# Four overflow blocks of an expert loop, moved from its end to places between its groups

## The reference, cut to what matters

```
def hier_moe(h, w_rg, b_rg, w_re, b_re, w_gate, w_up, w_down):
    ...                                  # choose 1 of 4 groups, then 2 of its 8 experts per token
    comb = jnp.einsum('tk,tke->te', gate, jax.nn.one_hot(eidx, N_EXPERTS, dtype=jnp.float32))
    a = jnp.einsum('td,edf->tef', t, w_gate)
    b = jnp.einsum('td,edf->tef', t, w_up)
    act = jax.nn.silu(a) * b * comb[:, :, None].astype(t.dtype)
    y = jnp.einsum('tef,efd->td', act, w_down)
```

## Time and profile before

| | |
|---|---|
| median of 3 runs | 1477.09 us (1475.53 to 1477.17) |
| the profiled execution's own time | 1473.9 us |
| its span in the trace | 1472.1 us |
| PE busy | 1273.6 us (87%) |
| DVE busy | 775.6 us (53%) |
| ACT, POOL busy | 283.2 us (19%), 150.3 us (10%) |
| DMA moved | 238.27 MB, mean 162 GB/s |
| expert loads (gate, up, down) | 36 of each, 1024 KB each |
| the loop, first gate-up product to the end of the last down product | 1061.19 to 1429.1 us |

### The profile page before, as it was taken

The page is one execution under the profiler, slowest core; times in us unless marked ns, Lnnn a source line. Parts: engine busy times, 40 slices in busy tenths (PEclk is TensorE's granted clock), DMA queues, the critical chain, the costliest instruction groups (busy, mean ns, idle before and its releaser), DMA issues.

```text
span 1472.1 us, 17784 instructions
## 1 busy us (share of the span) xinstructions
PE 1273.6 (87%) x6455; PEld 651.0 (44%) x6455; DVE 775.6 (53%) x2215; ACT 283.2 (19%) x812; POOL 150.3 (10%) x205
## 2 busy tenths in 40 slices
PE   7979699999999947787999999998599998899970
PEld 3435445554554433353555565655333433333430
DVE  1116789999898994231344445544435224434416
ACT  1123224433433341030111111111001110110100
POOL 0000001001100000100000000000100022132104
PEclk9998799999999968798999999998599999999995
DMA  8695000300000030372115110002379999999916
GB/s 329 245 351 181 1 22 1 143 30 16 14 29 15 1 141 29 128 264 115 29 43 215 43 43 15 1 15 100 127 297 384 356 407 418 417 416 416 389 67 222
DMA packets 68320, 238.27 MB, mean 162 GB/s; under 512 B 14112, under 2 KB 28358, under 8 KB 54387
## 3 DMA queue, kind: packets, MB, share of 16 engines
q1 hardware_dynamic: 56235, 217.20, 38.5%
q0 software_dynamic: 11424, 17.85, 3.5%
q10 hardware_dynamic: 576, 2.10, 0.4%
HBM read 216.27 MB, written 45.77 MB: 178 GB/s over the span
## 4 chain that ended last, share of the span: by engine, by line
PE 71%; DVE 13%; DMA 6%; issue 5%; ACT 2%; POOL 1%; SPq 1%; DVEq 0%; ACTq 0%; POOLq 0%
PE bank L777 24%; PE bank L1194 11%; PE bank L1147 9%; PE bank L1201 7%; DVE W L1605 6%; PE bank L976 3%; DMA W<-in_w_exp_down 3%; PE bank L1125 2%; PE bank L1085 2%; PE bank L820 2%; PE bank L1181 2%; DVE G L1550 1%; PE bank L889 1%; PE bank L1161 1%; DMA W<-in_cache_mem_k 1%
## 5 line engine op out<-in xcount | busy, mean ns | idle before, releaser
L777 PE MATMUL bank<-W,G 128*128 128x512 f32 (+3 forms) x864 | 354.0, 566 | 4.2 <-DVE G L1550 3.4
L1605 DVE SCALAR_TENSOR_TENSOR W<-W,dwT 128x128 f32<-128x128 f32 (+1 forms) x1080 | 280.3, 337 | 0.0
L777 PEld LDWEIGHTS bank<-W,G 128*128 128x128 f32 (+1 forms) x864 | 158.6, 187 | 176.2 <-issue 170.0
L1194 PE MATMUL bank<-W 128*32 128x512 f32 (+1 forms) x1600 | 204.9, 612 | 15.9 <-issue 14.2
L976 PE MATMUL bank<-W 128*128 128x512 f32 (+1 forms) x288 | 129.9, 610 | 11.7 <-DVE W L1711 7.8
L1194 PEld LDWEIGHTS bank<-W 128*32 128x32 f32 (+1 forms) x1600 | 65.4, 116 | 150.8 <-issue 148.4
L1147 PE MATMUL bank<-W 128*128 128x512 f32 (+1 forms) x288 | 128.2, 599 | 0.8 <-DVE W L1875 0.6
L659 POOL TENSOR_SCALAR st<-st 128x1 f32<-128x1 f32 (+5 forms) x58 | 13.2, 228 | 948.9 <-DVE st L1681 276.4
L1201 PE MATMUL bank<-W 128*32 128x512 f32 (+1 forms) x800 | 105.9, 610 | 4.1 <-DMA W<-in_w_exp_down 3.0
L2046 DVE TENSOR_TENSOR W<-bank,cvec 128x512 f32<-128x512 f32 x56 | 36.3, 687 | 131.3 <-PE bank L1181 131.2
L976 PEld LDWEIGHTS bank<-W 128*128 128x128 f32 (+1 forms) x288 | 54.0, 190 | 81.8 <-issue 81.6
(11 more groups left out here) (287 smaller groups left out, 1350.6 us busy)
## 6 DMA issues: line engine op xcount, KB each, us to landing
W<-in_w_exp_gate SPq DMA_DIRECT2D x36, 1024.0 KB, 11.5
W<-in_w_exp_up SPq DMA_DIRECT2D x36, 1024.0 KB, 15.6
W<-in_w_exp_down SPq DMA_DIRECT2D x36, 1024.0 KB, 15.5
y_scratch<-W SPq DMA_DIRECT2D x28, 512.0 KB, 12.7
y_scratch<-LG SPq DMA_DIRECT2D x1, 11264.0 KB
W<-in_cache_mem_k SPq DMA_DIRECT2D x8, 1024.0 KB, 5.3
W<-in_cache_mem_v SPq DMA_DIRECT2D x8, 1024.0 KB, 7.8
W<-in_w_in SPq DMA_DIRECT2D x4, 1792.0 KB, 25.1
```

The costliest lines, as they stand in the source:

```text
L777: mm = pe.matmul(bank[0:rows, at:at + hi - lo], HT[:, c, 0:rows], w[:, c, lo:hi], start=(c == 0), stop=(c == DC - 1))
L1194: mm = pe.matmul(B[2 + par][lo:hi, :], HG[par][:, c, lo:hi], WGU[u][:, :, c, :], start=(c == 0), stop=(c == DC - 1), skip_group_check=True)
L1605: dve.scalar_tensor_tensor(y, src, w, y, ALU.mult, ALU.add).then_inc(M["conv_tap"], 1)
```

## The change

The function `block_order` builds a list `BLOCKS`. It holds three expert blocks of each group, and behind the fourth, fifth, sixth and seventh group one overflow block. So the overflow blocks have the numbers 12, 16, 20 and 24 in the loop, and the last group's expert blocks are 25, 26 and 27. `block_column` gives the column of a block's rows in the index table, which keeps its old layout, and with it the place of its results in `y_d`. `weight_plan` walks the new order. The passes end with blocks 7 and 17 (7 and 15 before), and their combines go with blocks 10 to 15 and 20 to 25 (10 to 15 and 18 to 23 before). Two waits for the overflow table are added, on SP ahead of the read of an overflow block's expert number, and on GpSimd ahead of the first overflow block's row gather.

```
+def block_order():
+    order = []
+    for q in range(NE // 4):
+        order += [("e", 3 * q + r) for r in range(3)]
+        if 3 <= q < 3 + STATIC_OVER:
+            order.append(("o", q - 3))
+    return order
+
+
+BLOCKS = block_order()
+
+
+def block_column(n):
+    kind, k = BLOCKS[n]
+    return k if kind == "e" else NR + k
+
+
 def weight_plan():
-    need = []
-    for q in range(NE // 4):
-        need += [("e", 4 * q + 3)] + [("e", 4 * q + r) for r in range(3)]
-    need += [("o", k) for k in range(STATIC_OVER)]
-    uses = {}
-    for n in range(NR):
-        uses[n] = [("e", 4 * (n // 3) + n % 3), ("e", 4 * (n // 3) + 3)]
-    for k in range(STATIC_OVER):
-        uses[NR + k] = [("o", k)]
+    need, uses = [], {}
+    for n, (kind, k) in enumerate(BLOCKS):
+        if kind == "o":
+            uses[n] = [("o", k)]
+        else:
+            uses[n] = [("e", 4 * (k // 3) + k % 3), ("e", 4 * (k // 3) + 3)]
+        need += [w for w in reversed(uses[n]) if w not in need]
...
+        def pass_end(g):
+
+            return BLOCKS.index(("e", PER_PASS * (g + 1) - 1))
+
+        def stores_before(n, p):
+
+            return (n + 1 - p) // 2
+
         def comb_at(n):
 
-            g, j = n // PER_PASS - 1, 3 * (n % PER_PASS - 2)
-            return [] if g < 0 or g >= PASSES - 1 or j < 0 else [2 * NT * g + j + c for c in range(3)]
+            for g in range(PASSES - 1):
+                j = 3 * (n - pass_end(g) - 3)
+                if 0 <= j < 2 * NT:
+                    return [2 * NT * g + j + c for c in range(3)]
+            return []
...
                 if k not in over_e:
+                    sp.wait_ge(M["over_ready"], 1)
                     over_e[k] = sp.value_load(eid_i[0:1, k:k + 1], min_val=0, max_val=NE - 1)
...
-                gather(idx_i[:, n + 2:n + 3], zg_in[n % 2], ZG[n % 2])
+                if BLOCKS[n + 2] == ("o", 0):
+                    pool.wait_ge(M["over_ready"], 1)
+                at = block_column(n + 2)
+                gather(idx_i[:, at:at + 1], zg_in[n % 2], ZG[n % 2])
...
-                            pool.wait_ge(y_out[p], 16 * (PER_PASS // 2) * (g + 1))
+                            pool.wait_ge(y_out[p], 16 * stores_before(pass_end(g) + 1, p))
```

More of the change, by code:

```diff
@@ L597, in store_y @@
                 sp.wait_ge(M["yb_readyD"], n + 1)
-                g = min(n // PER_PASS, PASSES - 1)
-                sp.dma_start(y_d[g][(n - PER_PASS * g) * 128:(n - PER_PASS * g + 1) * 128, :], YB[n % 2]).then_inc(y_out[n % 2], 16)
+                at = block_column(n)
+                g = min(at // PER_PASS, PASSES - 1)
+                sp.dma_start(y_d[g][(at - PER_PASS * g) * 128:(at - PER_PASS * g + 1) * 128, :], YB[n % 2]).then_inc(y_out[n % 2], 16)
             over_e = {}
@@ L1184, in tiles_of @@
             def tiles_of(n):
-                if n >= NR:
+                if len(USES[n]) == 1:
                     return [(0, 128, WSLOT[USES[n][0]])]
```

## The result

| | before | after |
|---|---|---|
| median | 1477.59 us (7 runs, 1475.53 to 1481.47) | 1470.79 us (7 runs, 1467.23 to 1473.65) |
| profiled execution, its span | 1473.9, 1472.1 us | 1472.01, 1470.0 us |
| the loop, first gate-up to the end of the last down product | 1061.19 to 1429.14: 367.95 us | 1065.40 to 1425.89: 360.49 us |

The ratio of the changed kernel to the one before is 0.9949, with a 95% interval of 0.9933 to 0.9964: 6.8 us less. Two more comparisons of the same kernel gave 0.9935 (0.9908 to 0.9961) and 0.9954 (0.9937 to 0.9972). The forecast was 1469.6 us.

The account below looks back on a forecast made before the run. The full DMA stream was taken to bound the loop from 1178 us. Gain 9.7 - 1.7 - 0.5 = 7.5 us from the 1477.1 us median gave 1469.6 us, own range 1466 to 1473, wider range 1462.5 to 1475.5.

Parts of the forecast that it names:

- What bounds: Expert loop from 1178 us: the DMA byte stream, not TensorE, sets the pace; waits and slow products cost 22.3 us.
- check by bytes: Blocks 9 to 21 take 161.9 us, 140.2 without waits; their 66.62 MB need 160.5 us at 415 GB/s.
- The sum: Up to expert 28's weights: 48.6 us less TensorE work behind, 38.9 us more stream ahead; after small terms 7.5 us gained.
- main term of 9.7 us: Loop's end comes earlier by 48.6 us of TensorE work minus 38.9 us of added stream, before two small terms.
- The slow product at 25: Block 25's gate-up takes 8.77 instead of 7.05 us if TensorE waits over 3 us there: +1.7 us.
- The shape of the last blocks: Last three blocks become expert blocks of 32-column products, period 11.68 against 11.50 and 11.39 us: together +0.5 us.
- The small edits: SP's four expert-number reads (0.39 us each before), added overflow-table waits and moved combine gathers were costed at nothing.
- The signs: Right if DMA stays full until about 1380 us and waits sum to 12; wrong if loop's end moves under 4 us.
- an earlier issue doesn't make a full stream faster: For experts 17, 21 and 25, whose slots are freed three blocks ahead instead of two, no gain was counted.
- All waits go: Rival for TensorE's loop waits: longer issue distances clear them, gain up to 22.3 us, 1454.8 us; chance 0.10.
- The stream slows with the overflow loads in it: Rival for the loop's DMA: register-addressed loads run at 347 GB/s, no gain, 1477 us; chance 0.12 including moved waits.
- Late combine gathers: Rival for the second combine group: gathers landing after 20.7 us delay six steps by 2.0 us each, 1481.6 us; chance 0.06.

Follow-up runs that it names:

- the old order with the small loads: Kernel before, with the four overflow experts' loads cut to 64 columns of one chunk and no expert-number reads; ratio to before 0.9998, loop 368.85 us.
- the new one with them: Changed kernel, with the four overflow experts' loads cut to 64 columns of one chunk and no expert-number reads; ratio to before 0.9849, loop 347.34 us.
- the version with the pair behind the seventh group: Changed kernel with one overflow block moved from behind the sixth to behind the seventh group; ratio to before 0.9896, again 0.9919.

## Why the prediction was right

*What bounds.* Right: the stream sets the pace from 1178 us on. Without the overflow loads in it the waits went from 11.4 to 2.0 us. My "check by bytes" was none: 66.62 MB at 415 GB/s must give 160.5 us, since the rate was taken from the same stretch. It is the run without the loads that shows it.

*The sum.* I expected 16.15 MB more ahead of expert 28's weights; 16.50 came. I expected 38.9 us for them and block 25's gate-up 316.3 us after the first product (1377.5 - 1061.19). The time from block 9's product to that of the block that needs them grew by 39.0 us, and block 25's gate-up at 317.9 us (1383.34 - 1065.40). The difference of 1.6 us arose before block 9 (117.0 us against 115.5 from the first product), in the down product of block 5, which took 6.46 us in place of 4.94, at a granted clock of 0.50 until 1156 us where before it had risen after 1150 us (0.50, then 0.85). It is not of the change: a later profile of the kernel before has the same 117.0 us, and one of the new order 115.4. So the main term of 9.7 us was 48.6 - 39.0 = 9.6. That it agrees to 0.1 us is luck: in the other profiles of the two kernels the two times were 200.3 and 199.4 us, and 160.5 and 163.1, so the 39.0 could have been 36 to 40.

*The slow product at 25.* Right in the first profile: a wait of 3.84 us, 8.77 us of product. It is no fixed term, though: the second profile had 2.67 and 8.77, the third none there. And the second and third had waits of 4.06 and 4.41 us at block 13, with products of 9.68 and 8.62 us, where the first had 1.53 and 7.07. My sum has a slow product at block 25 alone.

*The shape of the last blocks.* 0.5 us was expected: periods of 13.37 us (a slow product in it) and 11.71 after block 25, against 11.50 and 11.39. The difference without the slow product is 0.5.

*A term that I didn't have.* The last down product took 5.40 us before and 3.64 after, 1.8 us for the change; the granted clock was 0.67 from 1424 us on before, and 1.00 there after. It was 5.40 in three of four profiles with the old order, and 3.64 in all three of the changed kernel. But it doesn't go with the order strictly: 3.70 in the old order with the small loads, 5.34 in the new one with them. It and the 1.6 us ahead of block 9 cancel, so the loop's 7.5 us is the forecast's 7.5 partly by luck. In the mean of all profiles the old order's loop is 368.7 us (367.95, 367.32, 370.70, and 368.85 with the small loads), the changed one's 359.2: 9.5 us, more than my 7.5 and just above the 9.2 that I gave for no slow product. The medians say 6.8, 8.0 and 6.8 us.

*The small edits.* SP's reads took less than before in the median, 0.28 us in place of 0.39:

```profile
L637 SPq TENSOR_LOAD <-eid_i x4: 263/275/476, 1189.5 to 1337.7; - x4
```

*The signs.* Most came: DMA share 1 until past 1380 us, waits of 11.4 us, the last for weights at block 25's gate-up with 3.84 us, none at the four overflow blocks' gate-up. Two did not. The stretch with little DMA at the end didn't shrink by about half: from 1403 us to the loop's end it was 26.1 us at a share of 0.10 before, and is 22.9 us at 0.16 now. And the loop's end moved by 3.2 us only (1429.14 to 1425.89), less than the 4 that I had called a sign of being wrong. The reason is the start, which came 4.2 us later, a difference between executions and not of the change; I should have named the loop's length.

*Where I was wrong.* The sentence that an earlier issue doesn't make a full stream faster is true for the stream, and misleads for one load: issued earlier it stands further ahead in the queue, and in the version with the pair behind the seventh group it landed 4.2 us earlier, in a loop that is 3.2 us shorter in the mean. It was one step outside my sum, and likely a better version than the one under study.

*The rivals.* "All waits go" needs the stream relieved by 12.5 MB; the order alone leaves 8 to 11 us. "The stream slows with the overflow loads in it": the rate ahead of block 25 was 416 GB/s, above the 414 before. The Trainium skill's limit of about 358 GB/s per core (DMA: Bandwidth & Descriptors, Specifications) was passed in both traces, in which this kernel used one core. "Late combine gathers" cost TensorE nothing: no wait of TensorE is named for them, and VectorE's longest was 1.8 us, within the 6.5 us that I gave it to spare.

## What to carry to other kernels

When the transfers are busy without a pause for a long stretch, ask which bytes stand in the queue ahead of the last load that an engine waits for, and how much work is left behind it. Work that needs few bytes belongs before that point, not behind it: at the end it only covers an idle DMA. Whether it is spread evenly or stands in a row matters less than that it comes before; and at the last wait, freeing the slot one block earlier moved that load past a store and 1 MB of other weights.

## What the runs showed of the hardware

The granted clock around the wait at block 25 of the changed kernel, in the columns of the earlier trace rows:

```profile
1379.00:1383.00 4.00, 0.50 (x8) 0.00 (x0) 2.61 (x4) 0.00 (x0) 1.98 (x2) 1.00 1.02 419
1383.00:1387.00 4.00, 3.66 (x20) 1.25 (x24) 2.26 (x2) 0.00 (x0) 0.00 (x0) 0.60 1.03 423
1387.00:1392.00 5.00, 5.00 (x48) 1.59 (x40) 0.00 (x0) 0.00 (x0) 0.00 (x0) 0.98 1.02 417
```

TensorE idled for 3.84 us, then worked at 0.60 of full speed on average over 4 us, which is a mix of the levels of 1.2 and 2.4 GHz, then at nearly 1. This wait cost its length and then 1.7 us (8.77 against 7.05). In all profiles, from block 1 on, gate-up products behind idle times of 2.67 to 5.53 us took 8.4 to 10.0 us, so 1.4 to 3.0 us more, and those behind 1.94 us or less took 7.05 to 7.08 (block 11's in the changed kernel's first profile, told above, was interrupted in itself). Down products don't part so cleanly: behind 1.88 us one took the usual 3.64, behind 1.90 and 2.09 us two took 5.30 and 5.24. So the same sum of waits costs less when it comes in small pieces. That part of a spread order's worth I had not counted.

The same program differs from run to run more than the change is worth: the kernel before took from 1471.54 to 1483.25 us in the comparisons and 1485.50 in a single execution, and the loop's start, in 14 profiles of nine kernels with the same code up to there, lies between 1061.19 and 1071.03 us. What decides that draw stays open; it was not tried.
